# A front that streams: input projection interleaved with its modulation, in a one-core diffusion step

## The chip, the cores and the metric

The kernel runs on one core of a Trainium2 chip. The metric is the device time of one execution in microseconds (us), the median of several runs. Engines are named as in the profile: PE is TensorE (PEld its weight loads), DVE is VectorE, ACT is ScalarE, POOL is GpSimd, SP is SyncE, which issues most DMAs.

## The reference, cut to what matters

One trunk layer over 640 tokens (512 latent, 128 context) of width 1024. Everything is float32.

```
sh1, sc1, g1, sh2, sc2, g2 = split(silu(cond) @ w_ada + b_ada, 6)      # two conditions: latent, context
h  = x * rsqrt(mean(x*x, -1) + EPS) * norm1 * (1 + sc1) + sh1
q, k, v, u = h @ w_in                       # 512 + 128 + 128 + 1024 columns
attention over q, k, v (per-head RMS norm, rotary turn);  conv module over u (gate, 31 taps, norm, silu, w_pw)
x  = x + g1 * (concat(attn, conv) @ w_out)
h2 = rms_norm(x, norm2) * (1 + sc2) + sh2
x  = x + g2 * peer(h2)                      # 16384 experts, top 16 of 8 heads
```

Only what makes `h` and multiplies it by `w_ada` and `w_in` concerns the change. The attention, the conv module's taps, the output projection and the expert layer stay as they are.

## The kernel before, in words

Features lie on the 128 partitions, tokens along the columns. `x` and `h` are 8 chunks of 128 features by 640 tokens. Every weight matrix is cut into blocks of 128 output columns (8 chunks of 128 x 128, 512 KB), which lie in HBM in the order of use, `wblk[0]` to `wblk[89]`. SP loads them all through one queue: the first 16 into 16 places of their own (`lead`, L334), the rest into a ring of 4 places (`ring`, `RING = 4`, L337 and L321). A ring place is loaded again only when the block that was in it has been used: block `at` waits in `load` for `blk_done >= at - RING + 1`, and `blk_done` counts the blocks that TensorE has finished, in their order. So 4 consecutive blocks are on the chip at most, the one in use among them.

The modulation (`ada`, L420) multiplies the two conditions by 48 blocks of `w_ada`. Four blocks make a group: their product is a row in a PSUM bank, ScalarE copies it (`copy_rows`, L805), and TensorE turns it into columns (`ada_turn`, L427), to which the bias is added (`read_mod`, L1071 on VectorE, or L835 on ScalarE). Groups 0 and 1 are shift 1, groups 2 and 3 scale 1, 8 blocks each, in the order of `w_ada`; VectorE reads all 16 columns at once, behind the turn of group 3.

The front, up to L1129, runs so. TensorE: group 0, the column sum of the 8 squared chunks (`column_sum`, with a matrix of ones), then groups 1, 2 and 3 with the turns of groups 0 to 3 between and behind them (all turns into bank 7). ScalarE: the squares of `x` in one instruction (L800), the copies, and, ahead of the copy of group 3, the square root (L812). VectorE: mean (L1083) and reciprocal (L1085) of the column sum, then `read_mod` for all 16 columns, two gains (L1076), and the products `h = x * gain * root` chunk by chunk (L1090, L1092), to which ScalarE adds the shift (L793, L794).

The projection has 14 blocks, `IN_KINDS`: `a` and `g` are the two halves of the conv input, `k`, `q`, `v` the attention's. Block b accumulates in `lin[b % 2]` over 8 chunks, each a matmul of 512 and one of 128 columns (L432, L433); ScalarE reads it out, and block b + 2 waits for that (`lin_act`). Block 0 waits for `h` chunk by chunk (`h_ready`). Behind block b, for b = 0 to 11, comes half a modulation group: two blocks of `w_ada`, `half_block(b)`, into bank 7. So the blocks in HBM come as 1 projection block, 2 modulation blocks, 1 projection block, and so on. Behind b = 2, 4, ..., 12 stands a turn, ahead of the half. Inside and behind some blocks stand small matmuls of the per-head norm (`root_sums` L475, `spread_root` L484) and of the rotary turn (`rotate` L492).

Meanwhile VectorE runs the conv taps: `gate(c)` (L1115) waits for the `a` and `g` block of its channel group, then 31 taps over 655 columns each (L1107), with the steps of the norm and of the rotary turn written in between, at fixed places (`inverse_root` L1134, `unit_root` L1140, `place_turn` L1149). It waits there for TensorE's small matmuls. Behind the projection the attention begins (L556).

The order of all this is written out by hand in each engine's own instruction stream; semaphores join the streams.

Of the kernel before, what the change touches and what calls it, by code (L numbers as in the profile page):

```python
# [78 lines left out]
S_ADA1, S_IN, S_PW, S_OUT, S_WQ, S_ADA3, S_END = 0, 16, 54, 58, 66, 82, 90  # L79
# [3 lines left out]
N_HALF = N_ADA2 // ADA_H  # L83

# [6 lines left out]

def in_block(b):

    return S_IN + b + ADA_H * min(b, N_HALF)


def half_block(i):

    return in_block(i) + 1


# [48 lines left out]
def build(nc, x_in, wblk, vecs, consts, kctx, vctx, keys, table, ublk, vtab, y_out, o_k, o_v):  # L150
    ctx = ExitStack()
    with ctx:
# [3 lines left out]
        def sem(name):  # L156
            return ctx.enter_context(nc.semaphore(name))
# [42 lines left out]
        lead = [view(5120 + 1024 * j, DC, P) for j in range(14)] + [view(21872 + 1024 * j, DC, P) for j in range(2)]  # L200
# [64 lines left out]
        squares = sem("squares"); sums = sem("sums"); sums_read = sem("sums_read"); inverse = sem("inverse"); root = sem("root"); piled = sem("piled")  # L265
# [16 lines left out]
        lead_in = [sem(f"lead_in{i}") for i in range(N_ADA1)]  # L282
# [31 lines left out]
        def _(sp):  # L314
# [25 lines left out]
            load(S_IN + RING, S_OUT - S_IN - RING)  # L340
# [63 lines left out]
        def _(pe):  # L404
            def weights(seq, i=None):

                if seq < N_ADA1:
                    pe.wait_ge(lead_in[seq], 16)
                    return lead[seq]
                n = 16 * ((seq - N_ADA1) // RING + 1)  # L410
# [41 lines left out]
            groups1 = N_ADA1 // ADA_G  # L452
            pe.wait_ge(ld_sel, 16)
            for g in range(groups1):
                ada(S_ADA1 + ADA_G * g, g)
                if g == 0:
                    pe.wait_ge(squares, 1)
                    column_sum(h, DC, 0)
                else:
                    pe.wait_ge(row_copied, g)  # L460
                    ada_turn(modrow[0][:, g - 1], 7, g - 1)
            pe.wait_ge(row_copied, groups1)
            ada_turn(modrow[0][:, groups1 - 1], 7, groups1 - 1).then_inc(ada_tp, 1)
# [23 lines left out]
            def rotate(c, turns):  # L487
                pe.wait_ge(znorm, c + 1)
                pe.wait_ge(mod_set, 1 + turns)
# [4 lines left out]
            for b, (kind, _) in enumerate(IN_KINDS):  # L494
                g = b // 2
                if b >= 2:
                    pe.wait_ge(lin_act, b - 1)
# [14 lines left out]
                else:  # L512
                    for c in range(DC):
                        if b == 0:
                            pe.wait_ge(h_ready, c + 1)
# [3 lines left out]
                        if c == 2 and b in TURN_IN:  # L519
                            rotate(TURN_IN[b], (b + 1) // 2 - 1)  # L520
# [7 lines left out]
                if b % 2 == 0 and g:  # L528
                    pe.wait_ge(row_copied, groups1 + g)
                    pe.wait_ge(mod_set, g)  # L530
# [3 lines left out]
                    ada_turn(modrow[1][:, (g - 1) % 2], 6, 0).then_inc(ada_tp, 1)  # L534
                if b == 0:
                    pe.wait_ge(mod_set, 1)
                if b < N_HALF:
                    ada(half_block(b), 7, ADA_H * (b % 2), ADA_H * (b % 2 + 1))
# [59 lines left out]
            pe.wait_ge(mod_set, 1 + N_MID)  # L598
# [6 lines left out]
            for un in range(N_UNITS):  # L605
# [5 lines left out]
                if un == SQ_UNIT:  # L611
                    pe.wait_ge(squares, 2)
# [29 lines left out]
            pe.wait_ge(mod_set, 1 + N_MID)  # L642
# [3 lines left out]
            def early_queries(j):  # L646
# [3 lines left out]
                for c in range(DC):  # L650
# [4 lines left out]
                    if j == 0 and c == 3:  # L655
                        pe.wait_ge(piled, DC - 2)
                        both(stat, ones[:], h[:, 0, :], 0, T_L, True, False)
                        pe.wait_ge(squares, 2 + DC)
# [45 lines left out]
            pe.wait_ge(row_copied, groups1 + (N_ADA2 + N_ADA3) // ADA_G)  # L704
# [11 lines left out]
            pe.wait_ge(mod_set, 2 + N_MID)  # L716
# [72 lines left out]
        def _(act):  # L789
            def add_shift(half, col):  # L790
                for c in range(DC):
# [8 lines left out]
            act.activation(h, x[:], ACT.Square).then_inc(squares, 1)  # L800
# [917 lines left out]
```

## Time and profile before

| what | us |
|---|---|
| median of 3 runs (1803.56 to 1804.62) | 1803.77 |
| profiled execution, its own time | 1804.06 |
| its span in the trace | 1802.3 |
| PE busy (94%) | 1689.0 |
| DVE busy (87%) | 1567.4 |
| ACT busy (43%) | 766.3 |
| POOL busy (37%) | 666.3 |

Times in the trace count from the start of the span. The front and the projection fill its first 196 us. The larger part of the span, from about 560 us on, is the expert layer, which the change does not touch. A busy share says little of a single stage; the rows below are from the stage that is changed. In a row of the order of time stand the start in us, the length in us, the engine, the line of the kernel, the operation with its output and input, the number of instructions merged in the row, and in brackets how long the engine had been idle and what ended that.

### The profile page before, as it was taken

How to read it: one execution, taken by the hardware profiler on the slowest of the kernel's cores; microseconds unless marked ns; L12 is line 12 of the kernel's file. 1: busy time of each engine (PE TensorE's matmuls, PEld its weight loads, DVE VectorE, ACT ScalarE, POOL GpSimd, SP SyncE). 2: the span in 40 equal slices, each digit the busy share in tenths (PEclk: the TensorE clock that was granted, in tenths of full speed). 3: DMA queues.
4: the chain of work that ended last, by engine and by line, in shares of the span. 5: the costliest groups of instructions: out<-in, count | busy, mean ns of one | idle time of the engine just before them, and what ended most of it. 6: DMA issues, size and time to landing. Idle time of an engine off the chain costs nothing.

```text
span 1802.3 us, 29022 instructions
## 1 busy us (share of the span) xinstructions
PE 1689.0 (94%) x9360; PEld 1418.1 (79%) x9360; DVE 1567.4 (87%) x3203; ACT 766.3 (43%) x1653; POOL 666.3 (37%) x659
## 2 busy tenths in 40 slices
PE   6999998999964886999999999999999999999997
PEld 4566776965543786889999998989999998999996
DVE  2687863389889997899999999999999999999999
ACT  3122463330003887444444444444444444444443
POOL 0000000035556886344444344344443444444441
PEclk9999999999985998999999999999999999999999
DMA  8444102211112688999999999999999999999996
GB/s 321 141 141 140 47 1 73 71 53 54 47 35 94 178 237 258 379 376 405 408 403 399 407 400 390 403 396 408 405 391 412 400 399 399 404 408 397 399 398 215
DMA packets 128782, 508.75 MB, mean 282 GB/s; under 512 B 8528, under 2 KB 63568, under 8 KB 79312
## 3 DMA queue, kind: packets, MB, share of 16 engines
q0 software_dynamic: 36864, 268.45, 37.0%
q1 hardware_dynamic: 91568, 239.37, 35.6%
q8 instruction: 35, 0.57, 0.1%
q14 instruction: 27, 0.22, 0.0%
q10 hardware_dynamic: 288, 0.13, 0.0%
HBM read 480.00 MB, written 27.92 MB: 282 GB/s over the span
## 4 chain that ended last, share of the span: by engine, by line
DVE 35%; DMA 21%; PE 21%; issue 19%; POOL 1%; ACT 1%; DVEq 1%; POOLq 0%; SPq 0%; ACTq 0%
DMA slab<-table,ixr 20%; DVE slab L1480 8%; PE psum L432 7%; DVE ulo L1394 4%; PE psum L638 3%; DVE slab L1432 3%; DVE slab L1472 3%; PE psum L725 2%; DVE vlo L1459 2%; PE psum L433 2%; DVE slab L1467 2%; DVE wlo L1455 2%; POOL slab L1569 1%; PE psum L569 1%; DVE slab L1436 1%
## 5 line engine op out<-in xcount | busy, mean ns | idle before, releaser
L1569 POOL DMA_INDIRECT slab<-table,ixr x256 | 425.2, 1661 | 603.6 <-DVE slab L1480 553.9
L746 PE MATMUL psum<-hhi,uhi 128*128 128x384 f32 x1008 | 339.5, 337 | 5.2 <-issue 5.0
L1480 DVE SCALAR_TENSOR_TENSOR slab<-slab,cf 128x1024 f32<-128x1024 f32 x256 | 328.2, 1282 | 14.7
L1472 DVE SCALAR_TENSOR_TENSOR slab<-slab,h2tok 128x1024 f32<-128x1024 f32 x256 | 311.9, 1218 | 31.5 <-DMA slab<-table,ixr 31.2
L746 PE MATMUL psum<-hhi,ulo 128*128 128x384 f32 x1008 | 338.7, 336 | 0.0
L746 PE MATMUL psum<-hlo,uhi 128*128 128x384 f32 x1008 | 338.1, 335 | 0.0
L760 PE MATMUL psum<-vhi,whi 128*128 128x512 f32 x768 | 300.0, 391 | 14.2 <-DVE wlo L1455 14.2
L760 PE MATMUL psum<-vhi,wlo 128*128 128x512 f32 x768 | 302.3, 394 | 0.0
L760 PE MATMUL psum<-vlo,whi 128*128 128x512 f32 x768 | 302.1, 393 | 0.0
L432 PE MATMUL psum<-slab 128*128 128x512 f32 x464 | 245.7, 612 | 7.9 <-ACT slab L881 5.2
L746 PEld LDWEIGHTS psum<-hhi,uhi 128*128 128x128 f32 x1008 | 189.8, 188 | 14.5 <-issue 9.8
L1012 ACT CAST whi<-slab 128x384 fp32r<-128x384 f32 x128 | 65.9, 514 | 308.9 <-DVE slab L1467 308.9
L746 PEld LDWEIGHTS psum<-hlo,uhi 128*128 128x128 f32 x1008 | 189.7, 188 | 4.2
L746 PEld LDWEIGHTS psum<-hhi,ulo 128*128 128x128 f32 x1008 | 189.6, 188 | 0.0
L433 PEld LDWEIGHTS psum<-slab 128*128 128x128 f32 x464 | 90.0, 194 | 115.0 <-issue 115.0
L760 PEld LDWEIGHTS psum<-vhi,whi 128*128 128x128 f32 x768 | 144.9, 189 | 41.8 <-issue 14.4
L760 PEld LDWEIGHTS psum<-vhi,wlo 128*128 128x128 f32 x768 | 144.7, 188 | 30.6
L760 PEld LDWEIGHTS psum<-vlo,whi 128*128 128x128 f32 x768 | 144.8, 189 | 27.9
L1459 DVE TENSOR_TENSOR vlo<-slab,vhi 128x1024 fp32r<-128x1024 f32 x128 | 156.0, 1219 | 9.4 <-ACT vhi L1004 9.4
L1018 ACT ACTIVATE ge<-av 128x1 f32<-128x1 f32 x256 | 52.0, 203 | 244.8 <-DVE slab L1472 244.8
L1394 DVE TENSOR_TENSOR ulo<-slab,uhi 128x1024 fp32r<-128x1024 f32 x128 | 155.9, 1218 | 0.0
L1551 POOL TENSOR_TENSOR hlo<-slab,hhi 128x3072 fp32r<-128x3072 f32 x1 | 6.7, 6684 | 379.8 <-ACT hhi L929 379.8
(210 smaller groups left out, 2662.2 us busy)
## 6 DMA issues: line engine op xcount, KB each, us to landing
slab<-ublk SPq DMA_DIRECT2D x64, 1024.0 KB, 8.7
slab<-vtab SPq DMA_DIRECT2D x64, 1024.0 KB, 8.7
slab<-wblk SPq DMA_DIRECT2D x90, 512.0 KB, 4.1
slab<-g_dram SPq DMA_DIRECT2D x32, 768.0 KB, 9.2
g_dram<-slab SPq DMA_DIRECT2D x11, 2048.0 KB, 8.7
slab<-table,ixr POOLq DMA_INDIRECT x256, 9.9
x<-x_in SPq DMA_DIRECT2D x1, 2560.0 KB, 9.5
y_out<-x SPq DMA_DIRECT2D x5, 512.0 KB, 3.5
```

The lines of the kernel that those rows point to most:

```text
L432: pe.matmul(dst[:, 0:512], w, src[:, l0:l0 + T_L], start=start, stop=stop)
L433: return pe.matmul(dst[:, 512:N], w, src[:, p0:p0 + T_P], start=start, stop=stop)
L638: last = pe.matmul(lin[j % 2][:, 512 * part:512 * part + half_cols], w[:, c, :], m[:, c, half_cols * part:half_cols * (part + 1)], start=( ...
L746: last = pe.matmul(psum[:, b, 0:ND], w[:, c, :], m[:, c, :], start=(m_ == 0), stop=(m_ == 3 * DC - 1))
L760: last = pe.matmul(psum[:, 2 + 2 * t + half, :], w[:, part], m[:, cols], start=start and k == 0, stop=stop and k == 2)
L1012: act.copy(whi[:, jj % 2, :], wgt[:, jj % 4, :]).then_inc(whi_set, 1)
L1394: v.tensor_tensor(ulo[:, jj % 4], uraw[:, jj // 2 % 2, jj % 2], uhi[:, jj % 2].bitcast(F32), ALU.subtract).then_inc(ulo_set, 1)
L1432: v.tensor_scalar(hot_b[:, b % 4, m, :], con[:, C_IOTA:C_IOTA + KEYS], e2T[:, col:col + 1], gT[:, col:col + 1], ALU.is_equal, ALU.mult)
L1459: v.tensor_tensor(vlo[:, jj % 4, :], vraw[:, jj // 2 % 2, jj % 2, :], vhi[:, jj % 2, :].bitcast(F32), ALU.subtract).then_inc(vlo_set, 1)
L1472: v.scalar_tensor_tensor(out=rows[:, sl % GR, 0:D], in0=rows[:, sl % GR, 0:D], scalar=1.0, in1=h2tok[:, k, :], op0=ALU.mult, op1=ALU.mult, ...
L1480: v.scalar_tensor_tensor(out=accs[k][:, e, :], in0=rows[:, sl % GR, D:2 * D], scalar=cf[:, sl:sl + 1], in1=accs[k][:, e, :], op0=ALU.mult, ...
L1569: pool.indirect_dma_start(out=rows[:, sl % GR, :], out_offset=None, in_=table, in_offset=bass.IndirectOffsetOnAxis(ap=ixr[:, half, sl % 8: ...
```

## The change: what it does

1. Groups 0 to 3 of the modulation are cut anew: group g now holds two blocks of shift 1 and two of scale 1, those of chunks 2g and 2g + 1. Each has a PSUM bank for its row (0, 1, 4, 6) and one for its turn (`TURN_BANK`). VectorE reads each pair by itself (`read_pair`) and makes the gains of its two chunks.
2. ScalarE squares `x` in four instructions of two chunks; VectorE adds them in two (chunks 0, 1 += 2, 3 and 4, 5 += 6, 7), and the column sum goes over 4 chunks in place of 8.
3. Behind the squares ScalarE takes the square root of one column into a tile that is written later anyway, and the copy of group 3 no longer stands near the square root.
4. Projection blocks 0 and 1 run together, chunk by chunk (`first_chunk`), with groups 2 and 3 and their turns between the chunks. Their weights are `wblk[12]` and `wblk[13]`, ahead of group 3's.
5. 18 blocks have places of their own in place of 16. The ring's first 4 loads wait together for the 4 blocks of group 0.
6. The 12 half groups no longer stand behind blocks 0 to 11 but behind blocks 2 to 11: one half each, and two behind block 6 and behind block 9 (`MID_HALVES`). The turns stand behind blocks 4, 6, 7, 9, 10 and 12 (`MID_TURN`), the row copies behind 3, 5, 6, 8, 9, 11 (`MID_COPY`), on ScalarE now after the turn's columns. `wblk` follows that order.

The rest of the diff renumbers semaphore counts (`mod_set` and `ada_tp` count the four pairs, `squares` one more).

```diff
-S_ADA1, S_IN, S_PW, S_OUT, S_WQ, S_ADA3, S_END = 0, 16, 54, 58, 66, 82, 90
+S_PW, S_OUT, S_WQ, S_ADA3, S_END = 54, 58, 66, 82, 90
+GROUPS1 = N_ADA1 // ADA_G
+ADA_SEQ = (0, 4, 8, 14)
+IN_SEQ = (12, 13)
+TURN_BANK = (7, 6, 7, 4)
+N_LEAD = 18
+MID_HALVES = {2: (0,), 3: (1,), 4: (2,), 5: (3,), 6: (4, 5), 7: (6,), 8: (7,), 9: (8, 9), 10: (10,), 11: (11,)}
+MID_COPY = {3: 0, 5: 1, 6: 2, 8: 3, 9: 4, 11: 5}
+MID_TURN = {4: 0, 6: 1, 7: 2, 9: 3, 10: 4, 12: 5}
 def in_block(b):
-    return S_IN + b + ADA_H * min(b, N_HALF)
+    return IN_SEQ[b] if b < 2 else N_LEAD + b - 2 + ADA_H * sum(len(MID_HALVES.get(a, ())) for a in range(b))
+def in_done(b):
+    return N_LEAD - 1 + b if b < 2 else in_block(b) + 1
...
-            for j in range(1, N_ADA1):
+            for j in range(1, N_LEAD):
                 sp.dma_start(lead[j], wblk[j]).then_inc(lead_in[j], 16)
-            for j in range(RING):
-                sp.wait_ge(blk_done, j + 1)
-                sp.dma_start(ring[:, j], wblk[S_IN + j]).then_inc(ring_in[j], 16)
+            sp.wait_ge(blk_done, ADA_G)
+            for at in range(N_LEAD, N_LEAD + RING):
+                sp.dma_start(ring[:, at % RING], wblk[at]).then_inc(ring_in[at % RING], 16)
...
+            def first_turn(g):
+                pe.wait_ge(row_copied, g + 1)
+                ada_turn(modrow[0][:, g], TURN_BANK[g], g).then_inc(ada_tp, 1)
+            def first_chunk(c):
+                pe.wait_ge(h_ready, c + 1)
+                for b in range(2):
+                    w = weights(IN_SEQ[b])
+                    last = both(lin[b], w[:, c, :], h[:, c, :], 0, T_L, c == 0, c == DC - 1)
+                    if c == DC - 1:
+                        last.then_inc(blk_done, 1)
+            ada(ADA_SEQ[0], 0)
+            pe.wait_ge(squares, 1)
+            for k in range(4):
+                if k == 2:
+                    pe.wait_ge(squares, 2)
+                last = both(stat, ones[:], h[:, 4 * (k // 2) + k % 2, :], 0, T_L, k == 0, k == 3)
+            last.then_inc(sums, 1)
+            first_turn(0)
+            ada(ADA_SEQ[1], 1)
+            first_turn(1)
+            pe.wait_ge(sums_read, 1)
+            ada(ADA_SEQ[2], 4)
+            first_chunk(0)
+            pe.wait_ge(mod_set, 1)
+            first_turn(2)
+            for c in range(1, 3):
+                first_chunk(c)
+            pe.wait_ge(mod_set, 2)
+            ada(ADA_SEQ[3], 6)
+            first_chunk(3)
+            first_turn(3)
+            for c in range(4, DC):
+                first_chunk(c)
...
-                if b % 2 == 0 and g:
-                    pe.wait_ge(row_copied, groups1 + g)
-                    pe.wait_ge(mod_set, g)
+                if b in MID_TURN:
+                    pe.wait_ge(row_copied, GROUPS1 + MID_TURN[b] + 1)
+                    pe.wait_ge(mod_set, GROUPS1 + MID_TURN[b])
...
-                if b < N_HALF:
-                    ada(half_block(b), 7, ADA_H * (b % 2), ADA_H * (b % 2 + 1))
+                for j, i in enumerate(MID_HALVES.get(b, ())):
+                    ada(half_block(b, j), 7, ADA_H * (i % 2), ADA_H * (i % 2 + 1))
...
-            act.activation(h, x[:], ACT.Square).then_inc(squares, 1)
+            for c in range(0, DC, 2):
+                act.activation(h[:, c:c + 2, :], x[:, c:c + 2, :], ACT.Square).then_inc(x_squared, 1)
+            act.wait_ge(ones_set, 1)
+            act.activation(nm[:, 0, 0:1], ones[:, 0:1], ACT.Sqrt)
...
+            copy_rows(ADA_G, modrow[0][:, 0], 0)
+            copy_rows(2 * ADA_G, modrow[0][:, 1], 1)
+            act.wait_ge(inverse, 1)
+            act.activation(rb[:, 0:N], rb[:, 0:N], ACT.Sqrt).then_inc(root, 1)
+            add_shift(0, M_SH1, range(1))
+            copy_rows(3 * ADA_G, modrow[0][:, 2], 4)
+            add_shift(0, M_SH1, range(1, 6))
+            copy_rows(4 * ADA_G, modrow[0][:, 3], 6)
+            add_shift(0, M_SH1, range(6, DC))
...
+            for k in range(2):
+                v.wait_ge(x_squared, 2 * k + 2)
+                v.tensor_tensor(h[:, 4 * k:4 * k + 2, :], h[:, 4 * k:4 * k + 2, :], h[:, 4 * k + 2:4 * k + 4, :], ALU.add).then_inc(squares, 1)
             inverse_mean(1, rb[:, 0:N], stat[:, 0:N], D)
-            read_mod(1, 7, N_ADA1, M_SH1)
-            norm_gain(0, M_SC1, V_NORM1)
-            rms_scale(0, 1)
+            for g in range(2):
+                read_pair(g)
+            rms_scale(0, 1, range(0, 4))
+            for g in range(2, 4):
+                read_pair(g)
+                rms_scale(0, 1, range(2 * g, 2 * g + 2))
...
+    pair_of = [np.r_[2 * g:2 * g + 2, DC + 2 * g:DC + 2 * g + 2] for g in range(GROUPS1)]
+    front = [ada[pair_of[0]], ada[pair_of[1]], ada[pair_of[2]], win[0:2], ada[pair_of[3]]]
+    for b in range(2, N_IN):
         front.append(win[b:b + 1])
+        for i in MID_HALVES.get(b, ()):
+            front.append(ada[N_ADA1 + ADA_H * i:N_ADA1 + ADA_H * (i + 1)])
```

`read_pair(g)` waits for `ada_tp >= g + 1`, adds the bias to the 4 x 2 columns of the pair in one instruction, and makes the gains of chunks 2g and 2g + 1 for both conditions in a second one.

## Rows read from the trace of the kernel before

**Rows 1.** The page's part 4, shares of the chain of work that ended last.

```profile
DVE 35%; DMA 21%; PE 21%; issue 19%; POOL 1%; ACT 1%; DVEq 1%; POOLq 0%; SPq 0%; ACTq 0%
```

**Rows 2.** Busy by engine (PE, PEld, DVE, ACT, POOL), clock, DMA share, GB/s.

```profile
60.00:196.00 136.00, 136.00 (x924) 89.16 (x913) 118.53 (x162) 28.66 (x64) 0.00 (x0) 1.00 0.39 132
```

**Rows 3.** The chain in order of time: start us, length us, what.

```profile
191.25 4.07 DVE slab L1107 x5
```

**Rows 4.** All engines in order of time, 11 to 39 us: start, length.

```profile
11.16 4.47 ACT L800 ACTIVATE slab<-x 128x5120 f32<-128x5120 f32 x1 [8.05 <-DMA x<-x_in]
...
16.34 2.07 PE L432 MATMUL psum<-slab,ones 128*128 128x512 f32 x2
...
21.13 1.02 PE L432 MATMUL psum<-slab,ones 128*128 128x512 f32 x2
...
26.85 0.82 DVE L1083 TENSOR_SCALAR slab<-psum 128x640 f32<-128x640 f32 x1 [26.85 <-PE psum L433]
27.71 4.15 DVE L1085 RECIPROCAL slab<-slab 128x640 f32<-128x640 f32 x1
...
32.12 1.28 ACT L812 ACT_TABLE_LOAD   x1
...
33.42 0.74 ACT L812 ACTIVATE slab<-slab 128x640 f32<-128x640 f32 x1
...
34.25 1.95 PE L427 MATMUL psum<-con,slab 128*128 128x2 f32 x16
...
36.23 0.19 DVE L1071 TENSOR_TENSOR mod<-psum,vec 128x32 f32<-128x32 f32 x1 [4.37 <-PE psum L427]
...
36.74 0.75 DVE L1090 SCALAR_TENSOR_TENSOR slab<-x,gain,slab 128x512 f32<-128x512 f32 x1
...
38.95 1.23 PE L432 MATMUL psum<-slab 128*128 128x512 f32 x2 [2.75 <-ACT slab L794]
```

**Rows 5.** Same columns as group 2: the loading of the leads.

```profile
16.00:34.00 18.00, 18.00 (x244) 12.54 (x240) 4.98 (x2) 3.62 (x5) 0.00 (x0) 1.00 1.03 409
```

**Rows 6.** A VectorE pass over 1310 columns, in order of time.

```profile
231.33 1.52 DVE L1234 TENSOR_TENSOR slab<-slab 128x1310 f32<-128x1310 f32 x1
```

**Rows 7.** The stretch of lowered clock, same columns as group 2.

```profile
39.86:43.28 3.42, 3.42 (x8) 1.86 (x7) 3.42 (x9) 3.42 (x8) 0.00 (x0) 0.51 0.00 0
```

**Rows 8.** TensorE in order of time, 56 to 71 us.

```profile
60.31 1.13 PE L432 MATMUL psum<-slab 128*128 128x512 f32 x2
...
69.07 0.95 PE L427 MATMUL psum<-con,slab 128*128 128x2 f32 x8
69.95 1.08 PE L420 MATMUL psum<-slab,scond 128*32 128x128 f32 x32
70.96 1.12 PE L432 MATMUL psum<-slab 128*128 128x512 f32 x2
```

**Rows 9.** ScalarE in order of time, 50 us.

```profile
50.34 1.28 ACT L826 ACT_TABLE_LOAD   x1
```

**Rows 10.** VectorE in order of time, 60 and 102 us.

```profile
60.21 0.69 DVE L1115 TENSOR_TENSOR slab<-slab 128x512 f32<-128x512 f32 x1 [15.77 <-ACT slab L827]
...
102.64 0.17 DVE L1134 TENSOR_SCALAR rr<-psum 128x10 f32<-128x10 f32 x1 [1.08 <-PE psum L475]
...
118.62 0.69 DVE L1149 TENSOR_TENSOR slab<-psum,con 128x512 f32<-128x512 f32 x1 [2.53 <-PE psum L492]
```

**Rows 11.** Landing of the one weight block issued at 69.4 us.

```profile
DMA to landing us min/median/max: 3.2/3.2/3.2
```

**Rows 12.** Landing of the next block, issued at 70.8 us.

```profile
DMA to landing us min/median/max: 4.1/4.1/4.1
```

**Rows 13.** Landing of all 37 blocks issued from 49 to 190 us.

```profile
DMA to landing us min/median/max: 3.1/4.5/6.5
```

**Rows 14.** TensorE in order of time, 147 to 149 us.

```profile
147.67 1.28 PE L475 MATMUL psum<-con,slab 128*128 128x2 f32 x10
148.80 1.10 PE L432 MATMUL psum<-slab 128*128 128x512 f32 x2
```

More of the change, by code:

```diff
@@ L199, in build @@
         keyT = view(9216, SB, P)
-        lead = [view(5120 + 1024 * j, DC, P) for j in range(14)] + [view(21872 + 1024 * j, DC, P) for j in range(2)]
+        lead = [view(5120 + 1024 * j, DC, P) for j in range(12)] + [view(28016 + 1024 * j, DC, P) for j in range(2)] + [view(c0, DC, P) for c0 in (17408, 18432, 21872, 22896)]
         z = view(11264, QK, N)
@@ L264, in build @@
         mod_set = sem("mod_set"); row_copied = sem("row_copied"); ada_tp = sem("ada_tp"); blk_done = sem("blk_done")
[L265 removed]
+        squares = sem("squares"); sums = sem("sums"); sums_read = sem("sums_read"); inverse = sem("inverse"); root = sem("root"); piled = sem("piled"); x_squared = sem("x_squared")
         scaled = sem("scaled"); h_ready = sem("h_ready"); lin_act = sem("lin_act"); lin_dve = sem("lin_dve"); spread = sem("spread")
@@ L281, in build @@
         kv_stored = sem("kv_stored")
-        lead_in = [sem(f"lead_in{i}") for i in range(N_ADA1)]
+        lead_in = [sem(f"lead_in{i}") for i in range(N_LEAD)]
         ring_in = [sem(f"ring_in{i}") for i in range(RING)]
@@ L488, in rotate @@
                 pe.wait_ge(znorm, c + 1)
-                pe.wait_ge(mod_set, 1 + turns)
+                pe.wait_ge(mod_set, GROUPS1 + turns)
                 if c:
@@ L519, in _ @@
                         if c == 2 and b in TURN_IN:
-                            rotate(TURN_IN[b], (b + 1) // 2 - 1)
+                            rotate(TURN_IN[b], sum(at < b for at in MID_TURN))
                         if c == 5 and b in SPREAD_IN:
@@ L789, in _, with add_shift @@
         def _(act):
-            def add_shift(half, col):
-                for c in range(DC):
+            def add_shift(half, col, chunks=range(DC)):
+                for c in chunks:
                     act.wait_ge(scaled, DC * half + c + 1)
@@ L1085, in inverse_mean, with read_pair, rms_scale @@
                 v.reciprocal(r, r).then_inc(inverse, 1)
-            def rms_scale(half, root_k):
+            def read_pair(g):
+                v.wait_ge(ada_tp, g + 1)
+                pair = slice(2 * g, 2 * g + 2)
+                bias = V(V_BADA, 2 * DC).rearrange("p (s c) -> p s c", s=2)[:, :, pair].unsqueeze(3).broadcast_to([P, 2, 2, 2])
+                v.tensor_tensor(mod[:, 0:2 * DC, :].rearrange("p (s c) k -> p s c k", s=2)[:, :, pair, :],
+                                psum[:, TURN_BANK[g], 2 * ADA_G * g:2 * ADA_G * (g + 1)].rearrange("p (s c k) -> p s c k", s=2, c=2), bias, ALU.add).then_inc(mod_set, 1)
+                v.wait_ge(mod_set, g + 1)
+                step(v.scalar_tensor_tensor(out=gain[:, 0, :, pair], in0=mod[:, M_SC1 + 2 * g:M_SC1 + 2 * g + 2, :].rearrange("p c k -> p k c"), scalar=1.0,
+                                            in1=V(V_NORM1 + 2 * g, 2).unsqueeze(1).broadcast_to([P, 2, 2]), op0=ALU.add, op1=ALU.mult))
+                settle()
+            def rms_scale(half, root_k, chunks=range(DC)):
                 v.wait_ge(root, root_k)
-                for c in range(DC):
+                for c in chunks:
                     v.scalar_tensor_tensor(out=h[:, c, 0:T_L], in0=x[:, c, 0:T_L], scalar=gain[:, half, 0, c:c + 1], in1=rb[:, 0:T_L],
@@ L1269, in _ @@
                 if j >= 2:
-                    v.wait_ge(squares, 2 + j)
+                    v.wait_ge(squares, 3 + j)
                     if j >= 3:
@@ L1666 @@
     win = blocks(a["win"][:, np.concatenate(order)])
-    front = []
-    for b in range(N_IN):
+    pair_of = [np.r_[2 * g:2 * g + 2, DC + 2 * g:DC + 2 * g + 2] for g in range(GROUPS1)]
+    front = [ada[pair_of[0]], ada[pair_of[1]], ada[pair_of[2]], win[0:2], ada[pair_of[3]]]
+    for b in range(2, N_IN):
         front.append(win[b:b + 1])
-        if b < N_HALF:
-            front.append(ada[N_ADA1 + ADA_H * b:N_ADA1 + ADA_H * (b + 1)])
-    wblk = np.concatenate([ada[:N_ADA1], *front, blocks(a["pw"]),
+        for i in MID_HALVES.get(b, ()):
+            front.append(ada[N_ADA1 + ADA_H * i:N_ADA1 + ADA_H * (i + 1)])
+    wblk = np.concatenate([*front, blocks(a["pw"]),
                            blocks(a["wout"][np.r_[pairs, qw:D]]), blocks(a["wq"]), ada[N_ADA1 + N_ADA2:]])
```

79 lines of the change are left out of this document (30 added, 49 removed).

## The prediction, written before the changed kernel was run

> **What bounds the kernel now.** I read the shares of the chain first, to see that no engine bounds the whole run: VectorE, the transfers and TensorE each hold a part [rows 1]. So the change is judged in its own stage. The busy times from 60 to 196 us show TensorE busy all 136.00 of 136 us at full clock [rows 2]: the projection ends when TensorE has got through its stream, and what is taken out ahead of it is won. VectorE is close behind; the chain passes through its taps for 4.07 us at 191 us [rows 3], so it has to start earlier by as much, or the gain ends there. In the order of time of the front the reader is to see why the first projection matmul starts only at 38.95: the turns of the last groups (34.25), the columns (36.23), the products (36.74), the shift, with TensorE idle for 2.75 us at the end [rows 4].
>
> **The front, step by step.** Until 16.34 us nothing changes: `x` is there at 11.16, and group 0 is done.
>
> - Squares: four instructions in place of 4.47 us in one. A 640-column square root takes 0.74, so about 0.83 ns a column; a 1280-column square is 1.26, the four end near 15.9. The two sums of pairs are 1280 columns, priced by a 1310-column pass of 1.52 [rows 6]: the second ends near 17.5. TensorE wants it only behind two chunk pairs, near 20, so all this is hidden.
> - Column sum over 4 chunks. In the row of before, the fourth pair starts at 21.13 and ends at 22.4; the eighth let VectorE start at 26.85 [rows 4]. Now VectorE starts at 22.55: 4.3 us earlier, not half of the sum, because the first two pairs run at the slow start and stay. Mean 0.82 and reciprocal 4.15 end at 27.55.
> - Root: before, the copy of group 3 and the table load of 1.28 stood ahead of 0.74 of work [rows 4]. The load now lies between squares and copy, near 16 to 17.3, hidden. Root done at 28.35. If a copy drove the table out again, 1.3 us would come back.
> - Meanwhile TensorE: turn 0 (1.0, half of the two turns at 34.25), group 1 (1.9, two halves as below), a wait of 0.7 for its copy (512 columns, by the 0.74 for 640), turn 1, group 2 to 28.7 [rows 4]. The queue moves 409 GB/s here, 1.28 us a block [rows 5]; the fourth block came about 1.0 ahead of the column sum's start at 16.34, so the twelfth comes at 25.5 (wanted at 27), the fourteenth at 28.1 (30.65), the eighteenth at 33.2 (38).
> - Pair 0 and 1 on VectorE: two small instructions each; 0.51 us for three from 36.23 to 36.74, so 0.85 for both pairs with their waits. Products start at 28.45. From there to the first projection matmul it was 38.95 - 36.74 = 2.2, so TensorE starts chunk 0 at 30.65, having waited 1.9.
>
> From 38.95 to 60.31 before lay 21.4 us: 16 chunk pairs, two half groups (2.0), and the clock loss: 3.42 us at 0.51 is 1.7 lost [rows 7]. So the 16 pairs are 17.3 with joints. From 30.65 now: 17.3, turns 2 and 3 (0.9 each, 69.07 to 69.95 [rows 8]) and group 3 (2.0, twice 69.95 to 70.96) = 21.1. Each chunk is delivered in about 0.93 us (0.75 for 512 columns [rows 4], a quarter more for 128) and used in 2.16, so TensorE doesn't wait again; pairs 2 and 3 are read 34 and 44 us in, each some 8 us ahead of need. Block 0's last matmul comes 1.08 ahead of block 1's, which covers its read-out (two instructions over 640 columns, about 0.9 by the root's 0.74): block 2 starts at about 51.9, against 60.31 [rows 8]: **8.4 us earlier**. But the two half groups that stood ahead of it (2.0) are still to come, so the front itself gives **6.4 us**. This counts on full clock throughout.
>
> VectorE's first gate needs block 1 read out: 51.9, a table load of 1.28 behind block 0's read-out [rows 9], then 0.9: near 54.0, against 60.21 [rows 10], 6.2 earlier. It keeps pace with the 6.4 to within 0.2.
>
> **The later blocks and the ring.** With H = 1.0 for a half and T = 0.9 for a turn, the new order does the same 12 and 6. Ahead of blocks 3 to 6, two halves and a turn less have been done, so they start 9.3 earlier. This helps nobody: VectorE is busy with taps, and only at 102.64 did it wait for TensorE's `root_sums` (1.08 us), then for `rotate` at 118.62 (2.53) [rows 10]. What counts is what happens at block 6 and at block 9, where two halves stand.
>
> There the ring is short. Four places hold block 6 and three of its four modulation blocks. The fourth is requested when block 6 is finished, and block 7 when the first modulation block is. Call t the start of the turn behind block 6. In the same situation before (t = 69.07), SP issued the first load at 69.4 and the next at 70.8, that is t + 0.35 and t + 1.75; they took 3.2 and 4.1 us to land [rows 11, 12]. So the fourth modulation block is there at t + 3.55, though wanted at t + 0.9 + 1.5 = t + 2.4: a wait of 1.2. Block 7 is there at t + 1.75 + 4.1 = 5.85; with the median landing of 4.5 [rows 13], which I take since more loads now follow, t + 6.25. Without a wait it would have started at t + 3.0. **Loss at block 6: 3.2 us**, both waits in it. At block 9 the same, but `root_sums` (1.13 by its start and the next one's [rows 14]) is done inside the wait: **2.1 us**. Before, every load had a whole projection block (8.7 us, 60.31 to 69.07 [rows 8]) to land, and all were hidden.
>
> These bounds come from the fastest and the slowest landing of 37, 3.1 and 6.5 [rows 13]: 1.85 + 0.75 = 2.6 us for both places, or 5.25 + 4.15 = 9.4. SP has only ring loads in its queue here, so nobody else waits for the waiting load; on TensorE the rest of the projection stands behind it, and VectorE at `place_turn` behind that.
>
> The Trainium skill (DMA: Bandwidth & Descriptors, the fit under the two cost components) gives a transfer about 2.0 us plus its bytes over 436 GB/s, hence 3.2 us by estimate for 512 KB. The row at 69.4 agrees, the one at 70.8, issued into a busy queue, does not (4.1). By the page's figure the two places would lose 2.8 together, and the sum would be -3.6 us.
>
> **Sum.** -6.4 + 3.2 + 2.1 = **-1.1 us** at the start of the attention. VectorE's waits behind block 9 are all for TensorE, so it follows. Later stages are chained to this one and are not changed. One more piece: moving row copies behind the turn's columns on ScalarE is hidden under blocks of 8.7 us. The profiled execution took 1804.06 (span 1802.3), 0.3 above the median; from it the forecast is 1803.0, for the median of runs 1803.77 - 1.1 = **1802.7**.
>
> **Rivals.**
>
> - *The transfer is hidden anyway*: refills at 6 and 9 arrive in time or nearly. For it: the transfers' share is only 0.39 in this stage [rows 2]. Against it: the wait is for a free place, not for bandwidth, and even the fastest landing leaves 2.6 us. It would give -6.4 to -3.8: 1797.4 at the full gain. 0.17.
> - *The clock falls in the new front.* TensorE now has idle stretches of 0.7 and 1.9 us between sparse turns, and the row of before shows that behind a sparse stretch with 2.75 us idle it was granted 1.2 GHz for 3.4 us [rows 7]. Once more costs 1.7: -1.1 + 1.7 = +0.6, 1804.4. 0.15. The Trainium skill (TensorE: Matmul & The Clock Gate, Part 1) says that the throttled state is the default and activity releases it, and that waits for transfers bring it back; the trace shows one such fall in the front, so the rule speaks for this rival, at the ring's waits too.
> - *The refills decide* (the other side): two halves behind one block outrun the ring. If block 7 and block 10 land as late as the slowest of the 37, the loss is 9.4, and the clock may fall in one of those waits of 4 to 5 us (1.7): -6.4 + 9.4 + 1.7 = +4.7, 1808.5. It decides from 6.4 us of loss on: the two places lose 2L - 3.65 for a landing time L, so from L = 5.0. For it: half of the 37 took 4.5 or longer; against it: both loads would have to be as slow as the slowest. 0.08.
> - *The early start is not got*: a table driven out or a late sum costs 1.3 or so: +0.2, inside my own range.
>
> **How the numbers follow.** Forecast 0.60, its own range 1800.8 to 1804.9. With the rivals, 1798.2 to 1806.0 leaves out most of the first one's full gain and of the third. About 0.2% (3.6 us) is what a measurement of this kernel tells from no change. Faster by more needs the ring's losses below 2.8 us: the first rival and a tail of mine, 0.22. Slower: the third, 0.08. Within: 0.70.
>
> **What would show it.** Reciprocal near 23.4; first projection matmul near 30.7; block 2 near 51.9; first gate near 54.0. Behind block 6 TensorE idle twice, waiting for the weights' transfer, about 1.2 and 2 us in all near 105 to 110, and again near 142 to 148; `place_turn` at 113.5; the attention's first rows some 1.1 earlier. The forecast is wrong if those waits are absent, if a stretch at 1.2 GHz lies at 30 to 50 us, or if the shift at the start of the attention is not the shift at the end.

## The result, and the profile after

| | before | after |
|---|---|---|
| median of 9 runs each | 1804.76 (1803.56 to 1807.96) | 1808.66 (1805.41 to 1809.82) |
| ratio | | 1.0019, 95% interval 1.001 to 1.0028 |
| profiled execution: time, span | 1804.06, 1802.3 | 1806.36, 1804.6 |

The change made the kernel slower by about 0.19%, where 0.06% faster was forecast, and its median lies above the range (1798.2 to 1806.0). Of the 6.0 us between the forecast of 1802.7 and the median, 1.0 is that the kernel before has a median of 1804.76 here, and had 1803.77 in the 3 runs that the forecast started from.

The page of the changed kernel (busy time by engine, then the chain's shares) hardly differs from that of before [rows 1]; nothing is to be found there.

```profile
PE 1682.3 (93%) x9344; PEld 1414.3 (78%) x9344; DVE 1571.0 (87%) x3210; ACT 766.6 (42%) x1657; POOL 665.5 (37%) x659
...
DVE 36%; DMA 20%; PE 20%; issue 20%; POOL 1%; ACT 1%; DVEq 1%; POOLq 0%; SPq 0%; ACTq 0%
```

The order of time of the front (start, length, engine, line; in brackets the idle time ahead and what ended it) shows that the front itself came out as worked out, and a little better: reciprocal at 22.86, root at 27.05, first projection matmul at 30.03 in place of 38.95 [rows 4], block 2 at 51.30 in place of 60.31 [rows 8], first gate at 53.30 in place of 60.21 [rows 10].

```profile
22.00 0.82 DVE L1128 TENSOR_SCALAR slab<-psum 128x640 f32<-128x640 f32 x1 [4.17 <-PE psum L447]
22.86 4.15 DVE L1130 RECIPROCAL slab<-slab 128x640 f32<-128x640 f32 x1
...
27.05 0.74 ACT L852 ACTIVATE slab<-slab 128x640 f32<-128x640 f32 x1 [1.76 <-DVE slab L1130]
...
27.91 0.75 DVE L1147 SCALAR_TENSOR_TENSOR slab<-x,gain,slab 128x512 f32<-128x512 f32 x1 [0.27 <-ACT slab L852]
...
30.03 1.12 PE L446 MATMUL psum<-slab 128*128 128x512 f32 x2 [1.75 <-ACT slab L833]
...
51.30 1.06 PE L446 MATMUL psum<-slab 128*128 128x512 f32 x2
...
53.30 0.69 DVE L1172 TENSOR_TENSOR slab<-slab 128x512 f32<-128x512 f32 x1 [8.01 <-ACT slab L871]
```

TensorE from 100 us on, in the same view. The "last turn" in what follows is the last rotary turn (`rotate`), which stands directly ahead of the attention; its start is the measure for the start of the attention. Behind block 6 stand the turn (t = 102.45), three modulation blocks (48 matmuls), 1.52 us idle for the weights of the fourth, that block, and 2.03 idle for the weights of block 7; behind block 9 it is 1.46, and 0.89 behind the small sums. The matmul pair at 110.20 takes 1.76 us, where the same pair took 1.02 elsewhere. The last turn starts at 197.87; before, it was 197.02 (the row by itself, from the trace of the kernel before).

```profile
103.33 1.52 PE L434 MATMUL psum<-slab,scond 128*32 128x128 f32 x48
106.37 0.65 PE L434 MATMUL psum<-slab,scond 128*32 128x128 f32 x16 [1.52 <-DMA slab<-wblk]
109.05 1.10 PE L446 MATMUL psum<-slab 128*128 128x512 f32 x2 [2.03 <-DMA slab<-wblk]
...
110.20 1.76 PE L446 MATMUL psum<-slab 128*128 128x512 f32 x2
...
143.94 1.52 PE L434 MATMUL psum<-slab,scond 128*32 128x128 f32 x48
146.92 0.64 PE L434 MATMUL psum<-slab,scond 128*32 128x128 f32 x16 [1.46 <-DMA slab<-wblk]
...
149.65 1.10 PE L446 MATMUL psum<-slab 128*128 128x512 f32 x2 [0.89 <-DMA slab<-wblk]
...
197.87 1.12 PE L533 MATMUL psum<-slab,con 128*128 128x512 f32 x2 [0.83 <-DVE slab L1203]
```

```profile
197.02 1.12 PE L492 MATMUL psum<-slab,con 128*128 128x512 f32 x2 [0.83 <-DVE slab L1140]
```

The window view (busy by engine, clock, DMA share, GB/s) of the stretch from 110.36 us shows why the pair is slow: TensorE was granted half its clock, 1.2 GHz, for 3.4 us.

```profile
110.36:113.77 3.41, 3.41 (x7) 1.47 (x6) 0.00 (x0) 0.00 (x0) 0.00 (x0) 0.50 0.33 133
```

The landing time of the fourth modulation block, requested when block 6 was finished, and then that of block 7, requested 1.4 us later (us from issue, where 3.2 and 4.1 stood in [rows 11, 12]):

```profile
DMA to landing us min/median/max: 3.5/3.5/3.5
```

```profile
DMA to landing us min/median/max: 4.7/4.7/4.7
```

VectorE in order of time: at `place_turn` it waits 7.25 us, 2.53 before [rows 10], and at `inverse_root` 3.67, where it was 0.34 before (the row by itself, from the trace of the kernel before). VectorE had come early and lost it nearly all at these two places.

```profile
115.11 0.69 DVE L1212 TENSOR_TENSOR slab<-psum,con 128x512 f32<-128x512 f32 x1 [7.25 <-PE psum L533]
...
148.81 0.17 DVE L1197 TENSOR_SCALAR rr<-psum 128x10 f32<-128x10 f32 x1 [3.67 <-PE psum L516]
```

```profile
148.98 0.17 DVE L1134 TENSOR_SCALAR rr<-psum 128x10 f32<-128x10 f32 x1 [0.34 <-PE psum L475]
```

So the front wins 9.0 us at block 2, of which 7.0 count, since two half groups (2.0) are only put off. At the attention nothing is left of it: the last turn is 0.85 us later.

### The profile page after: what moved, and what is told of

It is laid out like the page before. It is cut to its first block, busy times and chain, and to the rows that moved or that the text cites. A ratio compares the mean times of both kernels' runs of the same rounds, so it can differ in the third digit from the quotient of the medians.

```text
span 1804.6 us, 29014 instructions
## 1 busy us (share of the span) xinstructions
PE 1682.3 (93%) x9344; PEld 1414.3 (78%) x9344; DVE 1571.0 (87%) x3210; ACT 766.6 (42%) x1657; POOL 665.5 (37%) x659
## 4 chain that ended last, share of the span: by engine, by line
DVE 36%; DMA 20%; PE 20%; issue 20%; POOL 1%; ACT 1%; DVEq 1%; POOLq 0%; SPq 0%; ACTq 0%
DMA slab<-table,ixr 19%; DVE slab L1543 9%; PE psum L446 7%; DVE ulo L1457 5%; PE psum L677 3%; DVE slab L1495 3%; DVE slab L1535 3%; DVE vlo L1522 2%; PE psum L764 2%; DVE slab L1530 2%; PE psum L447 2%; DVE wlo L1518 2%; PE psum L608 1%; DVE slab L1499 1%; POOL slab L1632 1%
## 5 line engine op out<-in xcount | busy, mean ns | idle before, releaser
L1522 DVE TENSOR_TENSOR vlo<-slab,vhi 128x1024 fp32r<-128x1024 f32 x128 | 155.9, 1218 | 9.1 <-ACT vhi L1049 9.1
```

The costliest lines, as they stand in the source:

```text
L1522: v.tensor_tensor(vlo[:, jj % 4, :], vraw[:, jj // 2 % 2, jj % 2, :], vhi[:, jj % 2, :].bitcast(F32), ALU.subtract).then_inc(vlo_set, 1)
```

## The experiments

**The changed kernel again, unaltered.** No edit.

> The changed kernel once more, unaltered, to see how much of its extra time is the same from run to run. In its first profile block 2 began 9.2 us earlier than before, but TensorE waited 1.52 and 2.03 us for weights at block 6, 1.46 and 0.89 us at block 9, and its clock fell to half for 3.4 us right behind the first of these places; the attention began 0.85 us late. Theory A (ring shortage plus a clock fall behind it): the same four waits, within 0.3 us, and a fall behind at least one of the two places in every execution; attention late by -1 to +3 us; total 0 to 4 us above the kernel before. Rival B (the loss arises later, in the expert layer, and has nothing to do with the front): the attention is late by under 1 us and the total differs by over 2 us more than that.

Median 1807.64 against 1804.63 for the kernel before on the same chip, ratio on record 1.0008 (0.999 to 1.0025), which is not the quotient of the two medians; this sample alone does not tell the change from no change. TensorE in order of time has the same four waits, and the last turn at 198.20:

```profile
105.05 0.65 PE L434 MATMUL psum<-slab,scond 128*32 128x128 f32 x16 [1.43 <-DMA slab<-wblk]
107.78 2.04 PE L446 MATMUL psum<-slab 128*128 128x512 f32 x2 [2.08 <-DMA slab<-wblk]
...
145.59 0.64 PE L434 MATMUL psum<-slab,scond 128*32 128x128 f32 x16 [1.62 <-DMA slab<-wblk]
...
148.33 2.04 PE L446 MATMUL psum<-slab 128*128 128x512 f32 x2 [0.89 <-DMA slab<-wblk]
...
198.20 1.12 PE L533 MATMUL psum<-slab,con 128*128 128x512 f32 x2 [0.83 <-DVE slab L1203]
```

The windows at both places: at each of them the clock fell. At the first it fell within the second wait, at 107.3, before block 7 started at 107.78.

```profile
107.40:110.80 3.40, 3.02 (x5) 1.60 (x6) 0.00 (x0) 0.00 (x0) 0.00 (x0) 0.51 0.86 342
148.40:151.80 3.40, 3.40 (x6) 1.82 (x7) 2.72 (x4) 1.55 (x2) 0.00 (x0) 0.51 0.73 288
```

The waits belong to the change, not to one execution. The second fall cost another 1.7 us, which is why the last turn is no earlier, though this sample's first projection matmul was 1.2 us earlier (28.80). The expectation's 9.2 for block 2 is 9.0 by the rows (60.31 and 51.30).

**The kernel before again.** No edit.

> The kernel before once more, unaltered, as a control: how far two samples of one kernel lie apart, and where in the span their profiles drift apart. Theory A expects a ratio of 1 within 0.1% and the same times up to the attention within 0.3 us. Theory B expects drifts of 1 to 3 us in the expert layer (from 760 us on) between two profiles of one kernel.

Median 1804.21, ratio 0.9993 (0.9982 to 1.0003). Last turn at 197.95, 0.9 later than in the first profile: the clock fall in its front was 6.8 us long in place of 3.4. VectorE's instructions stay 0.8 to 0.9 us later up to 500 us and then drift against those of the first profile, from 1.9 us later to 3.1 us earlier in the expert layer. The ratio is as expected; the 0.3 us up to the attention was too strict.

**Six ring places.** The two new places are the columns that hold the keys later; the loads behind the projection return to four.

```diff
+DEEP = 6
+        deep = view(5120, DEEP, DC, P)
...
-            load(N_LEAD + RING, S_OUT - N_LEAD - RING)
+            for at in range(N_LEAD + DEEP, S_PW):
+                sp.wait_ge(blk_done, at - DEEP + 1)
+                deep_load(at)        # place (at - N_LEAD) % DEEP
+            load(S_PW, S_OUT - S_PW)
```

> The changed kernel with six ring places instead of four for the blocks of the projection (the two further ones lie where the keys are loaded later). Theory A: all four waits for weights are gone and the clock stays at full speed from 20 us to the attention; block 7 follows block 6 directly. The front's gain of 7.2 us (9.2 less two half groups) then reaches the attention: 6 to 7 us earlier than the kernel before, total about 1797 to 1799 where the kernel before has 1804. Rival B: the attention is 6 to 7 us earlier but the total is not, it stays within 2 us of the kernel before. Rival C (the waits are for transfer bandwidth, not for a free place): the waits remain, at over half their length.

Median 1797.29, ratio 0.9958 (0.9943 to 0.9973). In order of time, TensorE goes from the fourth modulation block (64 matmuls, none waited for) to block 7 without a gap, and the last turn starts at 190.46. The clock is 1.00 over the whole stretch in the window view:

```profile
30.79 1.13 PE L463 MATMUL psum<-slab 128*128 128x512 f32 x2 [1.74 <-ACT slab L850]
...
104.10 1.95 PE L451 MATMUL psum<-slab,scond 128*32 128x128 f32 x64
105.98 1.13 PE L463 MATMUL psum<-slab 128*128 128x512 f32 x2
...
190.46 1.12 PE L550 MATMUL psum<-slab,con 128*128 128x512 f32 x2 [0.83 <-DVE slab L1220]
```

```profile
21.00:196.00 175.00, 170.31 (x1296) 112.72 (x1295) 138.06 (x210) 44.75 (x97) 0.00 (x0) 1.00 0.44 160
```

Waits and falls are both gone, and the gain reaches the end: 6.56 us at the last turn (197.02 to 190.46), 7.3 between the medians (1804.63 to 1797.29). That no wait is left speaks against bandwidth: the same bytes go through the same queue in the same stretch of the kernel.

**The later order alone, on the kernel before.** The front and its ring loads are the old ones.

```diff
-    return S_IN + b + ADA_H * min(b, N_HALF)
+    return S_IN + b + ADA_H * sum(len(MID_HALVES.get(a, ())) for a in range(b))
...
-                if b < N_HALF:
-                    ada(half_block(b), 7, ADA_H * (b % 2), ADA_H * (b % 2 + 1))
+                for j, i in enumerate(MID_HALVES.get(b, ())):
+                    ada(half_block(b, j), 7, ADA_H * (i % 2), ADA_H * (i % 2 + 1))
```

> The kernel before with the later order of the changed one alone: no half group behind blocks 0 and 1, two behind blocks 6 and 9, turns and row copies as in the change; the front, the four ring places and the column sum over eight chunks are the old ones. Theory A: the same waits, some 3.5 us at block 6 and 2.3 us at block 9, and a clock fall of 1.7 us behind one of them: the attention is 5.5 to 8 us later than before, total 1809.5 to 1812. Rival C (the waits are for bandwidth) expects the same here; a rival by which the new front itself costs time (small instructions, more semaphores) expects under 3 us here.

Median 1814.09, ratio 1.0041 (1.0021 to 1.006). TensorE in order of time:

```profile
114.20 0.64 PE L423 MATMUL psum<-slab,scond 128*32 128x128 f32 x16 [2.43 <-DMA slab<-wblk]
115.56 2.05 PE L435 MATMUL psum<-slab 128*128 128x512 f32 x2 [0.71 <-DMA slab<-wblk]
...
153.06 0.65 PE L423 MATMUL psum<-slab,scond 128*32 128x128 f32 x16 [1.38 <-DMA slab<-wblk]
...
156.31 2.05 PE L435 MATMUL psum<-slab 128*128 128x512 f32 x2 [1.40 <-DMA slab<-wblk]
...
206.02 1.12 PE L495 MATMUL psum<-slab,con 128*128 128x512 f32 x2 [0.83 <-DVE slab L1144]
```

Waits of 3.14 and 2.78 us, 5.92 together, and two clock falls behind them (at 115.0 and 155.9 in the clock records): the last turn is 9.0 later than the 197.02 of the kernel before. The loss is in the new order, whatever the front does. The sum of the waits was as expected (3.5 and 2.3), its split was not. The delay of 9.0 lies above the expected 5.5 to 8, and the median above 1809.5 to 1812, since one clock fall was expected and two came.

**Five ring places.** As with six, `DEEP = 5`; the four blocks behind the projection also wait until the place that they overlap is used up.

> The changed kernel with five ring places for the projection's blocks. Theory A (a block waits for a free place, and is then 3.2 to 4.1 us on its way): the fourth modulation block behind blocks 6 and 9 has a place in time and isn't waited for; the projection block behind is requested when block 6 is finished, lands at t + 3.5 to 3.9 and is wanted at t + 3.0, so one wait of 0.5 to 1 us at block 6, none at block 9 (where the small sums cover it), and no clock fall: within 1.5 us of six places, total about 1798. A rival by which it is the number of loads in flight or their bandwidth expects waits of more than half of those with four places.

Median 1798.58, ratio 0.9958 (0.994 to 0.9976). One wait is left, 0.97 us at block 7, and no fall; the last turn is 160.68 us behind the first projection matmul (190.98 - 30.30), with six places 159.67.

```profile
106.53 1.10 PE L466 MATMUL psum<-slab 128*128 128x512 f32 x2 [0.97 <-DMA slab<-wblk]
...
190.98 1.12 PE L553 MATMUL psum<-slab,con 128*128 128x512 f32 x2 [0.83 <-DVE slab L1223]
```

That is the mechanism in a dose: each place more takes away just the waits that a free place decides.

**The waits filled with work.** Four places, and useless matmuls where TensorE waits.

```diff
+            def busy(b, n):
+                pe.wait_ge(lin_act, b)
+                for _ in range(n):
+                    pe.matmul(lin[(b + 1) % 2][:, 0:P], ones[:], h[:, 0, 0:P], start=True, stop=True)
...
+                        ada(half_block(b, j), 7, k, k + 1)
+                        busy(b, 6)
+                        ada(half_block(b, j) + 1, 7, k + 1, k + 2)
+                        busy(b, 8 if b == 6 else 3)
```

> The changed kernel with four places and with 14 (block 6) and 9 (block 9) added 128x128 matmuls of no use, placed where TensorE waits for the weights, about as long as the waits. Their result is overwritten. Theory A: the weights come at the same time as before, so the waits are filled but not shortened, block 7 and block 10 start within 0.5 us of where they did; the clock falls seen behind these places (one in one profile, two in the other, 1.7 us each) are gone: 1.7 to 3.4 us less than the changed kernel, total 1802 to 1805. A rival by which the clock falls have another cause (the small turns, the grid of the records) expects them unchanged and the total the same or 0.5 longer.

Median 1804.19, ratio 0.9994 (0.9981 to 1.0007). TensorE in order of time at block 6, and the last turn:

```profile
105.60 1.60 PE L431 MATMUL psum<-slab,ones 128*128 128x128 f32 x12
107.17 0.64 PE L439 MATMUL psum<-slab,scond 128*32 128x128 f32 x16
107.75 2.05 PE L431 MATMUL psum<-slab,ones 128*128 128x128 f32 x16
109.89 1.10 PE L451 MATMUL psum<-slab 128*128 128x512 f32 x2
...
196.68 1.12 PE L538 MATMUL psum<-slab,con 128*128 128x512 f32 x2 [0.83 <-DVE slab L1215]
```

First projection matmul (30.85) to last turn: 165.83 us, 6.16 above six places, against 8.17 in the first profile of the change (197.87 - 30.03) and 9.73 in the second. Block 7 starts as long behind the first projection matmul as in the first profile of the change (109.89 - 30.85 and 109.05 - 30.03, both 79.0), so the matmuls fill the wait and do not lengthen it. There is no clock fall before the attention. So the waits cost 6 us, and what comes on top is the clock: in the four profiles of the unaltered change it fell at 7 of these 8 places, here, with TensorE kept busy, at neither of the two. This is one profile; the median, at the kernel before's, agrees with it.

**Column sum over eight chunks.** Six places; `for k in range(DC)` in place of 4, and VectorE counts `squares` up without adding.

> Six places, but the column sum over all eight chunks again, without VectorE's two additions. Prediction's step: four further chunk pairs of 1.08 us each, all on the path to the reciprocal: first projection matmul 4.3 us later than with six places, attention 4.3 later, total about 1801.5. Rival: the four groups' matmuls and copies that now lie beside VectorE's reciprocal move too and something else becomes last, so that less than 3 us are lost.

Median 1800.97, ratio 0.9969 (0.9956 to 0.9983). First projection matmul and last turn in order of time:

```profile
35.40 1.12 PE L463 MATMUL psum<-slab 128*128 128x512 f32 x2 [1.74 <-ACT slab L850]
...
195.07 1.12 PE L550 MATMUL psum<-slab,con 128*128 128x512 f32 x2 [0.83 <-DVE slab L1220]
```

Both are 4.61 us later than with six places (30.79, 190.46). Not all of that is the sum: it began 0.45 later in this execution (16.84 against 16.39). From its start to VectorE's mean it was 10.54 us (to 27.38) against 6.38 (to 22.77), so the four pairs cost 4.2 us, near the 4.3 of four pairs at 1.08: all of them were on the path.

**Without the early square root.** Six places; the one-column `ACT.Sqrt` and its wait are taken out.

> Six places without the one-column square root behind the squares, which was there to fetch the table. Theory A: the table load then stands behind the copy of group 1, where ScalarE waits 1.76 us for the reciprocal and the load (1.28) needs no semaphore, so it is still hidden: the same time as six places within 0.3 us up to the attention. Rival: the load comes behind the wait, and everything is 1.3 us later.

Median 1796.80, ratio 0.9944 (0.9924 to 0.9964). ScalarE and VectorE in order of time, the first projection matmul and the last turn:

```profile
21.96 4.15 DVE L1145 RECIPROCAL slab<-slab 128x640 f32<-128x640 f32 x1
...
24.41 1.28 ACT L867 ACT_TABLE_LOAD   x1
...
26.15 0.74 ACT L867 ACTIVATE slab<-slab 128x640 f32<-128x640 f32 x1 [0.46 <-DVE slab L1145]
...
29.12 1.13 PE L463 MATMUL psum<-slab 128*128 128x512 f32 x2 [1.59 <-ACT slab L850]
...
188.79 1.12 PE L550 MATMUL psum<-slab,con 128*128 128x512 f32 x2 [0.83 <-DVE slab L1218]
```

The load begins right behind the copy of group 1, while the square root still waits, and is over before the reciprocal. A load on the path would show between the start of the reciprocal and the first projection matmul: that is 7.16 us here (21.96 to 29.12) and 7.16 with six places (23.63 to 30.79). Fetching the table ahead is worth nothing here. What hid the load is that the copy ahead of it now ends early (24.4); before, that copy began at 31.52, and load and root stood behind it.

**Two further samples of each kernel.** No edits.

> The changed kernel unaltered, a third sample, for the one thing still open: the attention began only 0.25 to 1.2 us late in two profiles, but the total was 3.4 us up in the first comparison (interval 1.8 to 5.1) and 1.4 in the second (-1.8 to 4.5). Theory A (waits 6 us, one or two clock falls of 1.7 behind them, and unchanged code behind the attention that varies by itself): last rotary turn at 196.5 to 199.5, one or two falls, and the time from there to the end anywhere from 1601 to 1608, as in other kernels with the same code there. Theory B (the change makes the later stages longer): that stretch is 1606 or longer each time, above that of the kernel before (1605.2 and 1605.0 so far).

> The kernel before unaltered, a third sample: last rotary turn at 197 to 198, one clock fall of 3.4 or 6.8 us in the front. Theory A: from there to the end anywhere from 1601 to 1608. Theory B: within 1 us of 1605.

> The changed kernel unaltered, a fourth sample. As for the third: theory A one or two falls behind the doubled places and a stretch behind the last rotary turn of 1601 to 1608; theory B 1606 or longer.

> The kernel before unaltered, a fourth sample. As for the third: theory A 1601 to 1608 behind the last rotary turn; theory B within 1 us of 1605.

The last turn in the third sample of the change, and in that of the kernel before, in order of time. The first, 200.08, lies above the expected 196.5 to 199.5.

```profile
200.08 1.12 PE L533 MATMUL psum<-slab,con 128*128 128x512 f32 x2 [0.83 <-DVE slab L1203]
```

```profile
197.11 1.12 PE L492 MATMUL psum<-slab,con 128*128 128x512 f32 x2 [0.83 <-DVE slab L1140]
```

All eight profiles (us; falls are stretches at 1.2 GHz before the attention):

| profile | first projection matmul | last turn | falls | from last turn to end |
|---|---|---|---|---|
| before, 1 | 38.95 | 197.02 | 3.4 in the front | 1605.2 |
| before, 2 | 39.21 | 197.95 | 6.8 in the front | 1605.0 |
| before, 3 | 39.03 | 197.11 | 3.4 in the front | 1605.7 |
| before, 4 | 39.63 | 198.45 | 6.8 in the front | 1607.0 |
| after, 1 | 30.03 | 197.87 | 3.4 at block 7 | 1606.7 |
| after, 2 | 28.80 | 198.20 | 3.4 at 7, 3.4 at 10 | 1607.9 |
| after, 3 | 30.33 | 200.08 | 3.4 at 7, 3.4 at 10 | 1604.6 |
| after, 4 | 29.57 | 199.31 | 3.4 at 7, 3.4 at 10 | 1605.5 |

The clock fell at 7 of the 8 doubled places in the change, and never there in the kernel before. On the average the change reaches the last turn 1.2 us later (198.87 against 197.63). Theory B falls: the stretch behind it was 1604.6 and 1605.5 in the new samples of the change, and 1607.0 in one of the kernel before, where 1605 to within 1 us was expected; the averages are 1606.2 and 1605.7. Theory A's width holds: this stretch took 1600.7 to 1608.2 over all 14 profiles of this study. Timings: ratios 1.0018 (1.0 to 1.0037) and 1.0034 (1.001 to 1.0057) for the change, 0.9997 and 1.0004 for the kernel before. All 36 runs of the change have a median of 1807.6, 116 of the kernel before 1804.6 (one far outlier of 4960 left out): +3.0 us (1.7 to 5.0, by resampling the runs).

## Why the prediction was wrong, point by point

- *The front* (6.4 us): right. Block 2 came 9.0 us earlier, so 7.0 with the two half groups taken off. The 0.6 more begins in the column sum: VectorE began at 22.00 and not 22.55, since the clock rose earlier (its first record is at 18.2 us, 19.3 before). That is luck: the same front began its projection anywhere from 28.80 to 30.85, and 30.65 was forecast. The two pairs were read in 0.7 us, but they did not decide; VectorE waited 0.27 us more for the root. With the ring's loss taken away (six places), the last turn was 6.56 us earlier than before, against 6.4 worked out.
- *Two slips in the front's working.* 21.4 less 2.0 and 1.7 is 17.7, not 17.3; the 17.3 that was used (16 pairs of 1.08) was the better number all the same, as block 2 began 21.27 us behind the first projection matmul, where 21.1 was worked out. And the copy that held up the square root before was that of group 2, at 31.52; group 3 was copied behind it.
- *Column sum*: 4.3 forecast, 4.2 when undone, apart from a later start. *Table load*: that the load was hidden now is right, but not by the early fetch; without it nothing was lost.
- *VectorE keeps pace*: right, 6.9 us earlier at the first gate, and it waited for TensorE at `place_turn` as foreseen, and at `inverse_root` behind block 9.
- *The ring*: right in mechanism, short in size. Forecast 3.2 at block 6 and 2.1 at block 9; measured 3.55 and 2.35 of waits. The first load landed in 3.5 in place of 3.2, block 7's in 4.7 in place of 4.5. With the joints it came to 6.16 us (waits filled), not 5.3.
- **The step that failed** is the sum "-6.4 + 3.2 + 2.1": it put the clock's loss behind the ring's waits at nothing, and it had the waits 0.9 us too short. The prediction let the clock fall in the ring's waits only in its third rival, "in one of those waits of 4 to 5 us", as in the front of before it had seen 2.75 us idle ahead of a fall. Waits of 1.4 to 1.6 and 2.0 to 2.1 us at block 6, with 0.65 us of modulation matmuls between them, were enough in 4 profiles of 4; 1.6 and 0.9 at block 9 in 3 of 4, and only 1.46 and 0.89 in the first profile were not. Each fall costs 1.7 us.
- *The sum with what was measured.* Without any loss by the ring the last turn stands 159.67 us behind the first projection matmul (six places). So the first profile's front had won 197.02 - 30.03 - 159.67 = 7.3 us, and the loss was 8.2: 0.85 later. The averages of four profiles each are 8.3 of gain and 9.5 of loss, 1.2 later; in part that gain is luck, as the front of before has 6.8 us of lowered clock in two of its four profiles. With the waits filled the last turn was at 196.68, still 0.3 earlier than in the first profile of before. So the falls decide the sign at the attention: the second rival's mechanism was at work, but at the third rival's place. That rival had 0.08; its 6.4 us of loss were passed by waits and clock together, not by landings as slow as the slowest.
- *The pages.* The Trainium skill (TensorE: Matmul & The Clock Gate, Part 1) says that waits for transfers bring the throttled state back. The traces agree, and the prediction named the ring's waits beside it, but had nothing for them in its sum. By the fit in the Trainium skill (DMA: Bandwidth & Descriptors, the fit under the two cost components) a load was to take 3.2 us by estimate, and the ring to cost 2.8; here the loads landed in 3.5 and 4.7, and 5.9 was waited. The rows were the better guide.
- *Rivals*: the hidden transfer is out, the free place decides (five and six places). The clock did not fall in the new front. The range was too narrow above: it held a clock fall or slow landings, hardly both.
- *Open*: the prediction called itself wrong if the shift at the attention is not the shift at the end, and that is so: 0.85 us at the last turn, 2.3 between the two profiled executions. The last turn accounts for 1.2 of the 3.0 us of the pooled timings, and not even that goes on: one and the same VectorE instruction some 500 us in (500.06, 500.89, 500.19 and 501.50 before; 499.86, 500.21, 502.40 and 502.10 with the change) is 0.5 us later on the average. The rest arises in the expert layer, which is not changed, and where two profiles of the kernel before drift by up to 4 us against each other. Why it should favour one side is not shown; four profiles of each kernel cannot tell it from chance.

Better than both is the change with six places and without the early square root: 1796.8 us, ratio 0.9944; with six places alone 0.9958. The two differ by less than their intervals.

## What to carry to other kernels

Count a prefetch ring in blocks between two long steps, not in bytes. A long step covers the landing of as many blocks as have a free place beside it. A block beyond that is requested only when a place comes free, and most of its landing is waited for (here 1.5 of 3.5 us and 2.0 of 4.7). Before moving short work together, ask what the longest run of short blocks is and give the ring that many places and two more, for the long block in use and for the long block behind the run: here four and two; with one place less, 0.97 us was still waited. And a wait on TensorE costs its length and can then cost the clock: price both, for waits of 1.5 us too.

## What the runs showed of the hardware that I had not expected

- The clock fell to 1.2 GHz for 3.4 us behind, or already within, two idle stretches of 1.4 to 1.6 and 2.0 to 2.1 us (4 profiles of 4), and behind 1.6 and 0.9 (3 of 3). It did not with 1.46 and 0.89, with one of 0.97 (five places) or with 0.7 and 1.75 in the front.
- The new front's first projection matmul lay anywhere from 28.80 to 30.85 us (eight profiles with the short sum). The two earliest, 28.80 and 29.12, are those in which the first record of the full clock is earliest, at 15.2 and 15.7 us; at 30.79 it is at 20.0.
- A table load does not wait with the instruction that needs it: without the early fetch it ran at 24.41, ahead of the square root's wait, and took 1.28 us. The next instruction started 0.01 us behind it where that had nothing to wait for (first profile of the change: load at 16.33, next at 17.62).
